# Reordered prologue: conditioning rows in a tile of their own, x loaded and turned first, parameter rows behind four modulation chunks

## The reference, cut to what matters

```python
mp = silu(c_ctx) @ w_mod[layer] + b_mod[layer]       # six vectors of 1024 for the prompt
ms = silu(c) @ w_mod[layer] + b_mod[layer]           # the same for the sample
hp = rms_norm(xp, norm1[layer]) * (1 + mp[1]) + mp[0]
hs = rms_norm(xs, norm1[layer]) * (1 + ms[1]) + ms[0]
z = h @ w_in                                         # layer 0: the first large product
```

## Time and profile before

| | |
|---|---|
| three runs | 2048.74, 2049.78, 2050.16 us (median 2049.78) |
| the profiled execution: span | 2050.2 us (nothing of it is listed outside its span) |
| busy share PE, DVE, ACT, POOL | 87%, 65%, 40%, 14% |
| mean granted TensorE clock | 0.931 of full |
| first matmul of the first large product | 83.91 us after the start |

### The profile page before, as it was taken

The page is one execution under the profiler, slowest core; times in us unless marked ns, Lnnn a source line. Parts: engine busy times, 40 slices in busy tenths (PEclk is TensorE's granted clock), DMA queues, the critical chain, the costliest instruction groups (busy, mean ns, idle before and its releaser), DMA issues.

```text
span 2050.2 us, 32403 instructions
## 1 busy us (share of the span) xinstructions
PE 1776.2 (87%) x11246; PEld 1594.4 (78%) x11247; DVE 1332.1 (65%) x2391; ACT 811.6 (40%) x1300; POOL 280.5 (14%) x280
## 2 busy tenths in 40 slices
PE   4898799999999999996477976798979799997992
PEld 1596399999999999992233764798968789997992
DVE  1587756568878784478885538344857678874445
ACT  1435424322122232322466333333744577753331
POOL 1000100000000000049910001002010122101012
PEclk9999899999999999995599998899989899998995
DMA  8333323446754351520000003336865799966334
GB/s 239 123 124 125 116 69 93 136 130 196 239 165 144 111 152 57 144 77 20 3 1 0 22 27 113 95 104 191 273 202 178 222 323 313 323 212 192 117 104 165
DMA packets 312644, 289.12 MB, mean 141 GB/s; under 512 B 20874, under 2 KB 301674, under 8 KB 312468
## 3 DMA queue, kind: packets, MB, share of 16 engines
q1 hardware_dynamic: 298292, 249.28, 39.3%
q0 software_dynamic: 12272, 34.50, 5.3%
q10 hardware_dynamic: 1904, 3.13, 0.5%
HBM read 263.38 MB, written 23.47 MB: 140 GB/s over the span
## 4 chain that ended last, share of the span: by engine, by line
PE 74%; DVE 11%; issue 7%; ACT 4%; DMA 2%; ACTq 1%; DVEq 0%; POOL 0%; POOLq 0%
PE ps L1264 19%; PE ps L1265 18%; PE ps L1266 18%; PE ps L1269 6%; PE ps L1270 3%; PE ps L1376 2%; DVE vp L2343 2%; PE ps L1307 1%; PE ps L1326 1%; DVE lo L1977 1%; ACT hi L770 1%; PE ps L1586 1%; PE ps L1701 1%; DVE hot L2579 1%; DMA y_rows<-rows_y 1%
## 5 line engine op out<-in xcount | busy, mean ns | idle before, releaser
L770 ACT ACTIVATE hi<-raw 128x1024 fp32r<-128x1024 f32 (+3 forms) x442 | 394.7, 919 | 559.6 <-PE ps L1266 474.3
L1977 DVE TENSOR_TENSOR lo<-raw,hi 128x1024 fp32r<-128x1024 f32 (+3 forms) x442 | 458.2, 1057 | 242.1 <-ACT hi L770 238.2
L1264 PE MATMUL ps<-h_wide,hi 128*128 128x320 f32 (+1 forms) x1728 | 542.0, 314 | 23.3 <-issue 17.1
L1265 PE MATMUL ps<-h_wide,hi 128*128 128x320 f32 (+1 forms) x1728 | 537.4, 311 | 0.0
L1266 PE MATMUL ps<-h_wide,lo 128*128 128x320 f32 (+1 forms) x1728 | 537.2, 311 | 0.0
L1264 PEld LDWEIGHTS ps<-h_wide,hi 128*128 128x128 f32 x1728 | 327.6, 190 | 26.3 <-issue 23.9
L1265 PEld LDWEIGHTS ps<-h_wide,hi 128*128 128x128 f32 x1728 | 327.4, 189 | 0.4 <-issue 0.2
L1266 PEld LDWEIGHTS ps<-h_wide,lo 128*128 128x128 f32 x1728 | 327.5, 190 | 0.0
L1264 PE MATMUL ps<-g_both,hi 128*128 128x320 f32 x528 | 166.7, 316 | 2.6 <-DVE g_both L2284 2.6
L1265 PE MATMUL ps<-g_both,hi 128*128 128x320 f32 x528 | 163.6, 310 | 0.0
L1266 PE MATMUL ps<-g_both,lo 128*128 128x320 f32 x528 | 163.6, 310 | 0.0
(11 more groups left out here) (381 smaller groups left out, 2825.8 us busy)
## 6 DMA issues: line engine op xcount, KB each, us to landing
raw<-in_moe_w_dram SPq DMA_DIRECT2D x160, 512.0 KB, 5.2
raw<-in_w_mod_dram SPq DMA_DIRECT2D x96, 512.0 KB, 4.5
raw<-in_moe_w_dram SPq DMA_DIRECT2D x96, 384.0 KB, 3.6
raw<-in_ff_w_dram SPq DMA_DIRECT2D x40, 512.0 KB, 4.7
raw<-in_moe_w_dram SPq DMA_DIRECT2D x64, 256.0 KB, 3.4
y_rows<-zeros POOLq DMA_DIRECT2D x22, 512.0 KB, 4.4
raw<-in_ev_w_in_dram SPq DMA_DIRECT2D x12, 512.0 KB, 5.8
raw<-in_ff_w_dram SPq DMA_DIRECT2D x16, 384.0 KB, 4.2
```

Source lines behind the costliest of these rows:

```text
L770: act.activation(hi[c % 2][:, parts[h]], raw[slot][:, parts[h]], ACT.Copy).then_inc(hi_done, 1)
L1264: pe.matmul(out, w_hi, v_hi, start=first, stop=False, skip_group_check=True)
L1265: pe.matmul(out, w_hi, v_lo, start=False, stop=False, skip_group_check=True)
L1977: dve.tensor_tensor(lo[c % 2][:, parts[h]], raw[ring_of(c) % 4][:, parts[h]], hi[c % 2][:, parts[h]].bitcast(F32), ALU.subtract).then_inc( ...
```

## The change

`c_ctx` and `c` get a tile `crow` of their own, loaded on ACT's queue right after `mats`; PE transposes it alone (16 rows) into PSUM bank 1, and ACT takes the silu straight from there. x is loaded first on SP's queue instead of on ACT's. The other 19 parameter rows move to SP's queue, behind chunks 0 to 3 of `w_mod` and ahead of chunk 4. The softplus, the router's split and the second weight's split move behind other steps. PE turns x first, then runs chunks 0 and 1, waits for the rows, turns them, runs the norm sum, then chunks 2 to 7.

```diff
@@ tiles, semaphores @@
+        crow = place("crow", [2 * KT, P], at=scratch + 4 * TT * D + 12 * P)
+        x_more_in = sem("x_more_in")
@@ SP @@
             def mods_before(n):
                 for q in range(2 * N_MOD):
+                    if q == 4 and n == 0:
+                        load_rows()
...
+            def load_rows():
+                sp.wait_ge(cleared, 1)
+                rows = [
...
+                for s, r, n, src in rows:
+                    sp.dma_start(prow[r:r + n, s, :], src).then_inc(rows_in, 16)
+                for r, src in ((QN, a["q_norm"]), (KN, a["k_norm"])):
+                    for h in range(2):
+                        sp.dma_start(prow[r:r + 1, 1, h * HD:(h + 1) * HD], src).then_inc(rows_in, 16)
+            for t in range(TT):
+                src = a["x_prompt"][0] if t == 0 else a["x_sample"][0, (t - 1) * P:t * P, :]
+                sp.dma_start(xrows[:, t, :], src).then_inc(x_in if t < 2 else x_more_in, 16)
@@ ACT @@
             act.dma_start(mats[:, :, :], a["const_mats"].rearrange("m p c -> p m c")).then_inc(mats_in, 16)
-            for t in range(TT):
...
-            act.wait_ge(prow_zero, 1)
...
+            act.dma_start(crow[0:KT, :], a["c_ctx"].rearrange("(c p) -> c p", p=P)).then_inc(mats_in, 16)
+            act.dma_start(crow[KT:2 * KT, :], a["c"][0].rearrange("(c p) -> c p", p=P)).then_inc(mats_in, 16)
-            act.wait_ge(par_kept, 1)
-            act.activation(cs[:, :, 0], par[:, 1, CX:CX + KT], ACT.Silu)
-            act.activation(cs[:, :, 1], par[:, 1, CS:CS + KT], ACT.Silu).then_inc(cs_silu, 1)
-            act.wait_ge(ab_lam, 1)
-            act.activation(sm[:, 1, :], sm[:, 0, :], ACT.Exp, scale=-1.0).then_inc(ex_lam, 1)
+            act.wait_ge(par_turned, 1)
+            act.activation(cs[:, :, 0], ps[:, 1, 0:KT], ACT.Silu)
+            act.activation(cs[:, :, 1], ps[:, 1, KT:2 * KT], ACT.Silu).then_inc(cs_silu, 1)
-            mod_row(0, 4)
...
-            mod_row(4, 2)
+            for k in range(4):
+                square(0, k, (x_kept, 10))
+            mod_row(0, 2)
+            for k in range(4, KT):
+                square(0, k, (x_kept, 10))
+            root(0)
+            mod_row(2, 2)
+            act.wait_ge(ab_lam, 1)
+            act.activation(sm[:, 1, :], sm[:, 0, :], ACT.Exp, scale=-1.0).then_inc(ex_lam, 1)
             act.wait_ge(small_in, 16 * 14)
             act.activation(wr_hi[:, :, :], wr_raw[:, :, :], ACT.Copy).then_inc(wr_h, 1)
-            squares(0, lambda k: (x_kept, 10))
-            root(0)
+            mod_row(4, 4)
+            mod_keep(0)
             split_hi(EIN)
-            split_hi(EIN + 1)
-            mod_row(6, 2)
-            mod_keep(0)
             shift_hi(0, 0, 0)
             for k in range(KT):
                 scaled_hi(0, 0, k)
+            split_hi(EIN + 1)
@@ PE @@
-            pe.wait_ge(mats_in, 16)
-            pe.wait_ge(rows_in, 16 * 21)
-            for s in range(3):
-                last = pe.transpose(ps[:, 5, s * P:(s + 1) * P], prow[:, s, :], ident)
-            last.then_inc(par_turned, 1)
-            pe.wait_ge(cs_silu, 1)
-            pe.wait_ge(mats_in, 16)
-            mods(0, 4)
-            pe.wait_ge(x_in, 16 * TT)
+            pe.wait_ge(mats_in, 16 * 3)
+            pe.transpose(ps[:, 1, 0:2 * KT], crow[:, :], ident[0:2 * KT, 0:2 * KT]).then_inc(par_turned, 1)
             for g in range(10):
                 t, q = g // 2, g % 2
+                if g == 0:
+                    pe.wait_ge(x_in, 16 * 2)
+                elif g == 4:
+                    pe.wait_ge(x_more_in, 16 * (TT - 2))
...
-            mods(4, 2)
+            pe.wait_ge(cs_silu, 1)
+            mods(0, 2)
+            pe.wait_ge(rows_in, 16 * 19)
+            for s in range(3):
+                last = pe.transpose(ps[:, 5, s * P:(s + 1) * P], prow[:, s, :], ident)
+            last.then_inc(par_turned, 1)
             norm_pe(0)
-            mods(6, 2, True)
+            mods(2, 6, True)
@@ DVE @@
             norm_rs(0)
+            dve.wait_ge(ex_lam, 1)
...
             split_lo(EIN)
-            split_lo(EIN + 1)
-            mod_params(0, part=0)
             shift_lo(0, 0, 0)
             for k in range(KT):
                 scaled_lo(0, 0, 0, k)
+            split_lo(EIN + 1)
```

More of the change, by code:

```diff
@@ L303, in hybrid_trunk_step @@
         evac = sem("evac")
-        prow_zero = sem("prow_zero")
-        ones_set = sem("ones_set")
+        cleared = sem("cleared")
         x_turned = sem("x_turned")
@@ L732, in _ @@
             act.dma_start(mats[:, :, :], a["const_mats"].rearrange("m p c -> p m c")).then_inc(mats_in, 16)
-            for t in range(TT):
-                src = a["x_prompt"][0] if t == 0 else a["x_sample"][0, (t - 1) * P:t * P, :]
-                act.dma_start(xrows[:, t, :], src).then_inc(x_in, 16)
-            act.wait_ge(prow_zero, 1)
[L737 to L760, removed]
+            act.dma_start(crow[0:KT, :], a["c_ctx"].rearrange("(c p) -> c p", p=P)).then_inc(mats_in, 16)
+            act.dma_start(crow[KT:2 * KT, :], a["c"][0].rearrange("(c p) -> c p", p=P)).then_inc(mats_in, 16)
             def split_hi(c, i=0, parts=WHOLE, fine=False, which=(0, 1)):
@@ L1978, in split_lo @@
                                       ALU.subtract).then_inc(lo_done, 1)
[L1980 to L1989, removed]
+            dve.memset(prow[:, :, :], 0.0).then_inc(cleared, 1)
+            dve.memset(ones[:, :], 1.0).then_inc(cleared, 1)
+            dve.memset(wg[:, :, :], 0.0).then_inc(cleared, 1)
             for g in range(0, 10, 2):
@@ L1996, in _ @@
                                 ps[:, X_BANKS[g % 3], :].rearrange("p (k c) -> p k c", k=4)).then_inc(x_kept, 1)
[L1997 to L2012, removed]
+            dve.wait_ge(par_turned, 2)
+            dve.tensor_copy(par[:, :, :], ps[:, 5, 0:3 * P].rearrange("p (s c) -> p s c", s=3)).then_inc(par_kept, 1)
+            dve.wait_ge(par_kept, 1)
+            dve.tensor_scalar(par[:, 1, QN:QN + 1], par[:, 1, QN:QN + 1], -HD ** -0.5, None, ALU.mult)
+            lam = par[:, 1, LAM:LAM + 8]
+            link(dve.tensor_scalar(sm[:, 2, :], lam, -1.0, None, ALU.mult))
+            dve.tensor_tensor(sm[:, 0, :], lam, sm[:, 2, :], ALU.max).then_inc(ab_lam, 1)
             def mod_params(g, part=None):
@@ L2115, in _ @@
             norm_rs(0)
+            dve.wait_ge(ex_lam, 1)
+            link(dve.tensor_scalar(sm[:, 3, :], sm[:, 1, :], 2.0, None, ALU.add))
+            link(dve.reciprocal(sm[:, 3, :], sm[:, 3, :]))
+            link(dve.tensor_tensor(sm[:, 3, :], sm[:, 1, :], sm[:, 3, :], ALU.mult))
+            link(dve.tensor_tensor(sm[:, 4, :], sm[:, 3, :], sm[:, 3, :], ALU.mult))
+            link(dve.tensor_scalar(sm[:, 5, :], sm[:, 4, :], 1.0 / 15, None, ALU.mult))
+            for odd in (13, 11, 9, 7, 5, 3):
+                link(dve.scalar_tensor_tensor(out=sm[:, 5, :], in0=sm[:, 5, :], scalar=1.0 / odd, in1=sm[:, 4, :],
+                                              op0=ALU.add, op1=ALU.mult))
+            link(dve.scalar_tensor_tensor(out=sm[:, 5, :], in0=sm[:, 5, :], scalar=1.0, in1=sm[:, 3, :],
+                                          op0=ALU.add, op1=ALU.mult))
+            link(dve.tensor_scalar(sm[:, 5, :], sm[:, 5, :], 2.0, None, ALU.mult))
+            link(dve.scalar_tensor_tensor(out=sm[:, 5, :], in0=sm[:, 2, :], scalar=0.0, in1=sm[:, 5, :],
+                                          op0=ALU.max, op1=ALU.add))
+            dve.tensor_scalar(sm[:, 6, :], sm[:, 5, :], 8.0, None, ALU.mult)
+            dve.tensor_scalar(sm[:, 7, :], sm[:, 5, :], -8.0, None, ALU.mult).then_inc(sp_ready, 1)
+            dve.wait_ge(wr_h, 1)
+            dve.tensor_tensor(wr_lo[:, :, :], wr_raw[:, :, :], wr_hi[:, :, :].bitcast(F32), ALU.subtract).then_inc(wr_l, 1)
+            mod_params(0, part=0)
             split_lo(EIN)
-            split_lo(EIN + 1)
-            mod_params(0, part=0)
             shift_lo(0, 0, 0)
@@ L2821, in _ @@
             pool.dma_start(wr_raw[:, :, :], a["moe_w_router"][0].rearrange("(k p) e -> p k e", p=P)).then_inc(small_in, 16)
-            pool.wait_ge(ones_set, 2)
+            pool.wait_ge(cleared, 3)
             for i, w in enumerate((a["a_w_r"], a["a_w_i"])):
```

20 lines of the change are left out of this document (17 added, 3 removed).

## The result

| | before | changed |
|---|---|---|
| median of the runs | 2049.97 us (2048.74 to 2051.63) | 2074.80 us (2073.54 to 2076.16) |
| ratio, 95% interval | | 1.0116 (1.0103 to 1.0128) |
| span of the profiled execution | 2050.2 | 2071.9 (its own time: 2073.54) |
| first matmul of the first product | 83.91 | 72.63 |
| mean granted clock | 0.931 | 0.925 |

What follows compares the result with a forecast made beforehand. The chain of waits up to PE's first large product was taken as the bound. 32.5 + 0.9 + 8.9 + 22.6 + 1.1 + 4.5 + 2.2 = 72.7 against 83.9, 11.2 us less: 2038.6 us, range 2034 to 2045.5.

Steps and rivals of the forecast that it cites:

- Part 1: Prologue ahead of the rows: x landed at 14 us, transposes done by 20, PE waiting for rows by 29.5, likely 27.
- Part 2: The 19 parameter rows on SP's queue: last issued at 30.5 us, rows landed at 32.5 (ends 30.5 and 37).
- Part 3: From rows landed to first product: transposes, norm sum, six chunks, tail and clock loss; first product at 72.7 us against 83.9.
- The tail behind `mod`: Between ACT's copy of `mod` and the first product: weight split, low parts and small gaps, 4.5 us.
- the clock: PE at half clock after standing for the rows: 2.2 us lost on the path, ends 0 and 4.5.
- Part 4, "what is moved at no cost": Second weight's split, softplus and POOL's clearing of `up` and `ub` move behind other steps without costing time.
- The first paragraph's inference: Chain from 84 to 177 us is 89% PE matmuls, without DMA: first product n us earlier, end n us earlier.
- a sign of being wrong: The forecast is wrong in the whole if the first product starts 11 us earlier and the end doesn't.
- Rival D: First product earlier but end not, as half-clock stretches of PE fall otherwise: 2048 to 2050 us, chance 0.06.
- C: Rival: SP stopped again among the small rows, rows at 46.7 us, 3.0 us slower, 2052.8 us; chance 0.05.
- The sum itself: Rows at 32.5 us plus the steps to the first product give 72.7 against 83.9, 11.2 us less: 2038.6 us.

Runs made afterwards that it cites:

- run 1: The changed kernel with 24 more instructions (48 already met waits) in ACT's program ahead of its silu: 2035.73 us, 0.9927 of before.

## Why the prediction was wrong

- **Part 1** (what lets PE begin) came out at its end, with some luck: x was there at 16.4 (14 said), its transposes done at 21.5 (20 at most was said) and PE's first chunk at 21.4 (19 said), but the two chunks took 7.1 us instead of 9.4, so that the second was through at 28.7 (27 to 29.5 said). All of it hid behind the rows.
- **Part 2** (when the rows land) was right: the last chunk issued at 22.5 as said, 19 issues in 7.7 us (8 said), the last landing 3.1 behind its issue (2 said), rows at 33.1 (32.5 said).
- **Part 3** was right to 0.7 us: from the rows to the first product 39.5 (40.2 said). The tail behind `mod` took 4.5 as said (PE stood 4.8); the clock cost 1.8 to 1.9 (2.2 said), 10.7 against 8.8 or 8.9 for the norm sum. That the sum of parts 2 and 3 hits 72.6 to 0.1 is luck: rows 0.6 too late and part 3 0.7 too short cancel. With the rows out of PE's way wait and clock together gave 7 us back, as the sum has it.
- **Part 4, "what is moved at no cost", is the step that failed.** It took the moved instructions by their time and their queues, not by the room they take in an engine's program, and so put the price of moving them at nothing. The 24 loads (19 of rows, five of x) left ACT's program, and the loop over experts slid over an edge. The price was three stalls of ACT of 11.3, 11.1 and 13.8 us, by which PE lost some 32: 36.2 us of waiting at its two lines against 6.9 before, and the granted clock of 0.50 and 0.56 in the 5 us behind the first two.
- **The first paragraph's inference** that a start n us earlier makes the end n us earlier rested on the chain up to 177 us. Behind it stood a stage with branches that depends on more than when it starts. The prediction had named this as a sign of being wrong ("the first product starts 11 us earlier and the end doesn't"), and it is what came. Rival D, the gain given back, named the right kind of outcome with the wrong mechanism (the clock) and a size too small; C, slower by rows on a held queue, did not happen.
- **The sum itself** was tried in run 1, where the code stands in its old place: 2035.7 against 2038.6, inside the range. That it beats the forecast by 3 us is not the prologue's work, as follows.

**Where the 3 us come from.** In run 1 the lead of 11.6 us at the first product is down to 6.4 by 1480 us, 13.0 at 1500 and 14.2 at 1650. Between 1480 and 1500 PE itself stands once with "issue". In the kernel before (1450 to 1525 us) and with 24 (1440 to 1512 us):

```profile
PE ps L1269 <- issue: 12.7, 1, 12.7
```

```profile
PE ps L1280 <- issue: 6.5, 1, 6.5
```

It is 12.7 and 12.5 us in the two runs with PE's program of before, and 6.5 to 7.6 in the other eleven, whether ACT's stalls are there or not. Without this run 1 would take some 2042 us (2035.7 and 6.2, an estimate), 3 us over the forecast and still inside the range: to come so near to it was in part luck. Why PE's stop is shorter is not shown.

**A fourth stall goes with the place of ACT's code.** From 1440 to 1515 us the change has

```profile
ACT L777 <- issue: 16.9, 1, 16.9
```

and the other runs with the three stalls 17.4 to 18.0 there, the kernel before and the runs without them 1.9 or less. Held against the run with 24, the change loses some 6 us of its lead between 1450 and 1600 us; held against the kernel before this is hidden, since PE's own stop is shorter. With the 32 us of the three stalls it makes up nearly all of the 39 us of run 1. Which branch of the loop stands there was not worked out.

Settled: the loss is the place of ACT's code against edges that lie 128 instructions apart. Open: where exactly the edge lies within twelve instructions, how many blocks ACT keeps and which part of a turn it fetches again (head, body and tail were moved together), and what PE's own stop depends on.

## What to carry to other kernels

ACT's program was fetched in blocks here, and moving instructions out of the straight part ahead of a loop with branches moves the whole loop against their edges. Where a trace shows an engine waiting for "issue" at a branch, look at the instruction queue in that stretch; then try a few instructions of padding before an edit is judged, since here 24 that do nothing turned +1.2% into -0.7%. And a step that starts behind a wait for late data should be asked what of it needs that data: the norm sum needed none.

## What the runs showed of the hardware

- ACT's code came in packets of 8 KB (the queue's packets came and went with ACT's padding alone). Where a turn through the loop's smallest body touches three blocks of 128 instructions, there were 2 fetches or fewer in the 160 us of the stretch and no such stall; where it touches four or more there were 13 to 15 (17 in 175 us of the change) and three stalls of 11 to 14 us. The Trainium skill (Runtime: NRT & Kernel Launch, Instruction fetch mechanics) says that most engines' instruction memory holds two lines of 16 KiB, 256 instructions each, and that a taken branch out of this window waits for a fetch. The traces agree with the stall; with two lines of 256 they don't, since with 152 instructions of padding, 128 more than 24, the body would cross an edge of such lines, and it was as fast (2034.95 and 2035.73 us).
- Met waits aren't free. An instruction of two of them took ACT 0.08 us: 280 of them took 22 us, from the landing of `crow` at 9.2 to ACT's table load at 31.2; 232 took 18.5 us, from ACT's last row at 18.4 to its table load at 36.9. The 232 outlasted ACT's 9.5 us of idle time and made PE's first chunk 9.0 us later (38.57 against 29.57).
- The eight loads on SP's queue ended their issue at 22.5 us in both kernels, with five more DMAs of x ahead of them in one.
